# Respreading the projection's matmul pieces over the steps of a top-k search, in a hybrid attention layer

## The reference

```python
h = layer_norm(concat(meta, x))                     # 2064 x 1024
proj = h @ w_in                                     # qa ka va | qb cb | qi ki wi | gates (2 x 1024)
k_idx = layer_norm(ki); c_kv = rms_norm(cb)
rel = relu(einsum('bqhd,bsd->bqhs', qi, k_idx))     # indexer, 8 heads
score = einsum('bqh,bqhs->bqs', w_idx, rel)         # masked by chunk
top_idx = top_k(score, 256)                         # per query; then attention over those keys
y_a, y_b = window_attention(...), attention_over_gathered(...)
h = layer_norm(alpha*h + (sigmoid(gA)*y_a + sigmoid(gB)*y_b) @ w_out)
h = layer_norm(alpha*h + (silu(h @ w_gate) * (h @ w_up)) @ w_down)
```

## Time and profile before

| | |
|---|---|
| median of 3 runs | 3820.75 us (3813.96 to 3821.17) |
| the profiled execution's own time | 3810.51 us |
| its span | 3808.3 us, 2.2 us less than its time |
| granted PE clock, mean | 0.961 |
| busy share of the span: PE, PEld, DVE, ACT, POOL | 92%, 77%, 57%, 50%, 46% |

### The profile page before, as it was taken

How to read it: one execution, slowest core, us unless ns; L and a number is a source line. 1 busy time by engine, 2 the same in 40 slices (tenths; PEclk the granted TensorE clock), 3 DMA queues, 4 the chain that set the end, 5 groups by cost and what they waited for, 6 DMA issues and landing times. The chain is left out here.

```text
span 3808.3 us, 52394 instructions
## 1 busy us (share of the span) xinstructions
PE 3509.4 (92%) x17866; PEld 2927.4 (77%) x17866; DVE 2166.8 (57%) x2906; ACT 1900.5 (50%) x3569; POOL 1743.3 (46%) x2034
## 2 busy tenths in 40 slices
PE   6998788898989999999997998999999999999896
PEld 5876566676767888988996876778887888888685
DVE  4206666787522366567442665774547545466857
ACT  3213577787634698888554332343334333344342
POOL 6213566666411232222102665656665666554544
PEclk9988899899987999999998999999999999999998
DMA  7324222432231111100003455754536443465562
GB/s 249 145 71 111 79 75 70 159 84 83 83 98 39 37 40 43 35 26 15 19 15 136 148 171 200 237 194 139 180 138 202 149 149 136 153 246 188 212 226 95
DMA packets 327960, 464.22 MB, mean 122 GB/s; under 512 B 22808, under 2 KB 216552, under 8 KB 323848
## 3 DMA queue, kind: packets, MB, share of 16 engines
q1 hardware_dynamic: 301296, 417.88, 33.2%
q10 hardware_dynamic: 26400, 43.00, 3.2%
HBM read 307.02 MB, written 153.78 MB: 121 GB/s over the span
## 5 line engine op out<-in xcount | busy, mean ns | idle before, releaser
L2465 POOL TENSOR_TENSOR ff_rounded_ring<-ff_raw,ff_rounded_ring 128x512 fp32r<-128x512 f32 x264 | 383.6, 1465 | 288.2 <-ACT ff_rounded_ring L2601 285.4
L99 PE MATMUL ff_bank<-ff_rounded_pair,ff_rounded_ring 128*128 128x512 f32 x1232 | 483.2, 392 | 14.1 <-POOL ff_rounded_ring L2465 9.0
L100 PE MATMUL ff_bank<-ff_rounded_pair,ff_rounded_ring 128*128 128x512 f32 x1232 | 481.6, 391 | 0.0
L101 PE MATMUL ff_bank<-ff_rounded_pair,ff_rounded_ring 128*128 128x512 f32 x1232 | 481.6, 391 | 0.0
L1647 PE MATMUL at_ctx<-at_p_t,at_c_nat 128*128 128x128 f32 (+1 forms) x2432 | 350.7, 285 | 7.8 <-ACT at_ctx_t L1760 7.0
L1647 PEld LDWEIGHTS at_ctx<-at_p_t,at_c_nat 128*128 128x128 f32 (+1 forms) x2432 | 305.7, 194 | 37.3 <-ACT at_ctx_t L1760 12.9
L1754 ACT ACTIVATE at_p_t<-at_turn 128x512 f32<-128x512 f32 (+4 forms) x416 | 213.1, 544 | 207.0 <-PE at_turn L1624 173.5
L2470 POOL TENSOR_TENSOR ff_rounded_ring<-ff_raw,ff_rounded_ring 128x512 fp32r<-128x512 f32 x154 | 214.9, 1401 | 187.2 <-ACT ff_rounded_ring L2651 187.1
L99 PEld LDWEIGHTS ff_bank<-ff_rounded_pair,ff_rounded_ring 128*128 128x128 f32 x1232 | 232.6, 189 | 66.1 <-POOL ff_rounded_ring L2465 11.8
L2832 DVE TENSOR_TENSOR ff_rounded_a_ring<-ff_f_q,ff_rounded_a_ring 128x512 fp32r<-128x512 f32 x154 | 199.2, 1301 | 135.8 <-ACT ff_rounded_a_ring L2643 134.6
L101 PEld LDWEIGHTS ff_bank<-ff_rounded_pair,ff_rounded_ring 128*128 128x128 f32 x1232 | 232.5, 189 | 48.6
(11 more groups left out here) (360 smaller groups left out, 9106.4 us busy)
## 6 DMA issues: line engine op xcount, KB each, us to landing
f_kept<-ff_resid SPq DMA_DIRECT2D x154, 256.0 KB, 2.5
ff_f_q<-f_kept SPq DMA_DIRECT2D x14, 2816.0 KB, 10.1
pj_raw<-in_w_in SPq DMA_DIRECT2D x50, 512.0 KB, 4.5
proj<-se_row SPq DMA_DIRECT2D x96, 256.0 KB, 2.2
ff_raw<-in_w_ff_gate SPq DMA_DIRECT2D x22, 1024.0 KB, 10.7
ff_raw<-in_w_ff_up SPq DMA_DIRECT2D x22, 1024.0 KB, 6.3
ff_raw<-down_comb SPq DMA_DIRECT2D x88, 256.0 KB, 2.7
ff_raw<-in_w_ff_down SPq DMA_DIRECT2D x66, 256.0 KB, 3.2
```

The lines of the kernel that those rows point to most:

```text
L99: pe.matmul(out, lhs_lo, rhs_hi, start=start, stop=False, skip_group_check=goes_on)
L100: pe.matmul(out, lhs_hi, rhs_hi, start=False, stop=False, skip_group_check=goes_on)
L101: return pe.matmul(out, lhs_hi, rhs_lo, start=False, stop=stop, skip_group_check=goes_on)
L2465: pool.tensor_tensor(ring[:, step % RING, 1, :].rearrange("p (k c) -> p k c", c=P), f_operand(it, q, m), f32(ring[:, step % RING, 0, :]).r ...
```

## The change

The estimate of a search step's other work grows by 2600 columns for the time that hand-overs between engines take. The pause after piece 384 is one step instead of three. In the second half a step has at most 7 pieces instead of 8, except in the last eight steps. And the last two chunks of the first half are ordered by group: both units of group 2, then both of group 3.

```diff
-RELOAD_STEPS = 3
+RELOAD_STEPS = 1
...
-    units = [(c, g, k) for k, c in enumerate(OTHERS) for g in (2, 3)]
+    many = len(OTHERS)
+    units = [(c, g, k) for k, c in enumerate(OTHERS[:many - 2]) for g in (2, 3)]
+    units += [(OTHERS[k], g, k) for g in (2, 3) for k in (many - 2, many - 1)]
...
-        tally = 2 * width(2 * q + 2) + 600 if 0 <= q < LATE - 1 else 0
+        tally = 2 * width(2 * q + 2) + 3200 if 0 <= q < LATE - 1 else 0
...
-        steps[n] = range(done, done + min(many, KT))
+        steps[n] = range(done, done + min(many, KT if done < many_in_all // 2 or n > LAST_STEP - HEADS else KT - 1))
```

## The result

The changed kernel takes 3795.17 us (median of 5 runs, 3792.6 to 3799.87) against 3817.21 us for the one before, run beside it (5 runs, 3812.41 to 3821.17): a ratio of 0.995 with a 95% interval of 0.9939 to 0.9962. A second comparison gave 3797.33 against 3816.31 us, again 0.995 (0.9937 to 0.9964). It is faster by 19 to 22 us where 10 were forecast. The absolute time, 3795 us, lies just under the range of 3798 to 3825 us. That range was built on a median of 3820.75 us for the kernel before; as a share of it, it begins at 0.994, and 0.995 lies inside. The profiled execution took 3798.26 us, with a span of 3796.0.

What follows compares the result with a forecast made beforehand. PE was taken to bound steps 80 to 95, the searches round DVE, POOL and ACT steps -8 to 79. Terms -11.6 - 3 + 2.5 + 1 + 1 = -10.1 us, from 3820.75 to 3810.6 us; range 3798 to 3825 us.

Steps and rivals of the forecast that it cites:

- the main term: Steps 80 to 95 lose 17 pieces at 0.68 us with PE never idle: -11.6 us, at least zero.
- The end zone gives nothing: Rival, chance 0.05: another engine sets the pace in the last steps, or the stage's end hangs elsewhere; +1.5 us, 3822 us.
- About half should show: -3, bounds 0 and -6.1: Steps -34 to -9 lose 9 pieces, 6.1 us of PE; about half shows because ACT also waits for DVE.
- +2.5, +1 and +1: Costs forecast for units' extra ACT and POOL work, for key blocks in neighbouring steps, and for the reload's wait.
- the mark of 6 us: Sign against the forecast: the middle stretches more than 6 us longer in sum.
- the other mark: Sign against the forecast: ACT waits for PE in the middle stretches.
- Key blocks: Three pairs of key units complete in neighbouring steps, so PE waits for DVE's normalising: +1 us, bounds 0 and 6.6.
- The wait for h in step 42: PE waits 2 to 5 us for the reload's group 1, expected 13 us after issue; cost +1 us, bounds 0 and 5.
- The searches pay for the pieces: Rival, chance 0.20: POOL's 12 more quarters and ACT's copies lengthen steps -8 to 47, up to 17.8 us; +5.2 in sum, 3826 us.
- Units out of step with the loop: Rival, chance 0.10: units beginning mid-step wait for an accumulator, steps 41 to 89; at 0.6 us a step +19 us, 3840 us.
- More comes back than counted: Rival, chance 0.12: steps 48 to 79 give 5.5 us, the first stretch its whole 6.1; -18.7 us, 3802 us.

Runs made afterwards that it cites:

- key_block_earlier: Changed kernel with 8 pieces moved from steps -8 to -1 into -16 to -9, so a further key block is made before step -8; 3802.13 us, ratio 0.9984.
- pieces_earlier: Changed kernel with 6 pieces moved from steps -8 and -7 into -34 to -9, same key units completed there; 3801.96 us, ratio 0.998.
- handover_4500: As handover_and_reload, but with the estimate's constant at 4500 in place of 3200; 3767.17 us, ratio 0.9891 to the kernel before.
- all_but_order: The whole change but with the old order of the units; 3792.85 us, ratio 0.9949 to the kernel before.
- keys_apart: Changed kernel with 12 pieces moved from steps -4 to 5 into 7 to 18, so no two key units complete in neighbouring steps; 3799.82 us, ratio 0.9976.
- all_but_seven: The whole change without the limit of seven, so up to 8 pieces a step in the second half too; 3781.76 us, ratio 0.9918 to the kernel before.
- only_reload: Kernel before with only the pause shortened from three steps to one; 3804.11 us, ratio 0.998.
- handover_and_reload: Kernel before with the larger estimate and the one-step pause, old unit order, up to 8 pieces a step; 3771.63 us, ratio 0.9902.
- only_handover: Kernel before with only the larger estimate for the searches' steps (3200 in place of 600); 3783.04 us, ratio 0.9921.
- same_as_after: The changed kernel run and profiled again with no edit, beside the kernel before; 3797.33 us, ratio 0.995.

## Why the prediction was right, and where not

**The direction was right, and so was the main term.** 17 pieces fewer at the end gave 115.0 - 103.4 = 11.6 us, as forecast. It holds far beyond this case: 128, 112, 111, 88, 72 and 64 pieces take 115.0, 104.1, 103.4, 87.6, 76.7 and 71.6 us, with PE idle nowhere by more than 0.15 us. "The end zone gives nothing" is out.

**The sum is nearer than its parts.** The first stretch gave 7.2 us more than forecast, steps 48 to 79 gave 2.1 more, and the middle cost 4.3 more. These errors partly cancel, and that is luck: -15.1 us by the stretches, where -10.1 was forecast.

**The step that failed: "About half should show: -3, bounds 0 and -6.1".** Steps -34 to -9 gave 10.2 us. That is beyond its bound, because the bounds knew of pieces only. With 5 units instead of 6 a whole key block leaves the stretch, with its chain over PE, ACT, POOL and DVE. Put back with 8 pieces (key_block_earlier), the stretch takes 74.0 us, as long as before. The table of the change had the 6 and the 5. How the 10.2 us split isn't shown. At 0.65 us a piece the nine pieces would be 5.9 us and the block 4.3, but 0.65 is the most that pieces_earlier allows, and handover_4500 doesn't follow such a sum: with 3 pieces and one completed unit fewer than after, the stretch takes 70.1 us. The waits of ACT for DVE in the earlier trace rows were read as a sign that pieces are half covered; no run measures that half.

**Steps -8 to 47 cost 8.8 us, not the 4.5 forecast** (+2.5, +1 and +1). That passes the mark of 6 us that the prediction set itself, and ACT does wait for PE there (8.2 and 2.2 us), the other mark. But the largest term isn't among those named. The new order was priced at nothing and costs 8.7 us in steps 24 to 39; all_but_order, without it, is 5.2 us shorter than before there, in spite of 9 pieces more. Steps -8 to 7 cost 3.2, of which a key block moved in from the first stretch would be 3.1. Steps 8 to 23 cost 2.6 and steps 40 to 47 give 0.5. The wait that the term "Key blocks" named is there, and larger than its bound of 6.6: 9.7 us on PE for DVE's normalising, where before had 3.0. But moving the units apart didn't shorten the stretch (keys_apart), so its price of 1 us isn't confirmed. The wait for h in step 42 is 0.3 us, not 2 to 5. The load was sized fairly, 13.6 to 14.6 us from issue to landing against the 13 taken; PE came to step 42 later than forecast, after a wait of 7.1 us for line 926 at the start of step 41. What caused that one isn't shown.

**"The searches pay for the pieces"** doesn't hold. ACT's waits for POOL's judgements were 33.8 and 13.3 us, and are 32.6 and 12.6, with 12 quarters more on POOL in the middle. 39 pieces more in all_but_seven cost 7.9 us, 0.2 each, against 0.68 at the end. The 16 pieces of only_reload cost 1.3 us net, the 16 of handover_and_reload against only_handover 3.1. PE's waits for line 926 gave way, 30 us in the middle where 39 were forecast.

**"Units out of step with the loop"** was given 0.10, and its mechanism is in the trace. PE waits for the accumulator of two units earlier in 4 of the 49 steps, 10.9 us in all, hidden under "issue"; so a unit that begins within a step does meet an evacuation that ACT does at its step's end. It also waits for the next chunk's low part, an operand that the rival didn't name: 14.1 us in the middle, 8.8 in steps 48 to 79. What was wrong is the price: steps 48 to 79 got 2.1 us shorter in spite of these waits, and nothing near 0.2 us a step was lost. Steps 59 and 61, with waits of 3.5 and 4.1 us, take 11.2 and 14.0 us where before took 7.6 and 8.4, but their neighbours are shorter. Only the 6.7 of step 36 are shown to cost.

**"More comes back than counted"** (3802 us) is nearest to what happened: 2.1 us in steps 48 to 79, where its quarter was 5.5, and more than the whole 6.1 of the first stretch. 32 pieces fewer are 21.8 us of PE's work there: 12.7 of it became idle time (24.9 to 37.6), about 7 went into longer matmuls (the granted clock is 0.95 where it was 0.97), and 2.1 is gained. PE's waits for line 926 didn't rise by 20 us; they fell from 29.5 to 17.5, and waits for low parts (8.8) and for evacuations (10.9) took their place.

**What stays open.** The stretches account for -15.1 us; the ratio says 19 us, with an interval of 14.5 to 23. The difference seems to lie in the runs of before. Beside after and same_as_after their medians are 3817.21 and 3816.31 us; in the second of these comparisons eight of the nine ran at a granted clock of 0.956 to 0.958 and the ninth, at 0.961, took 3806.65 us. Beside all other versions the medians are 3809.22 to 3811.34 us, at 0.960 on average. Against those, after's two medians are 12 to 16 us faster, which fits the stretches. Why the clock was lower there isn't known. That after gains no more than this on such a chip isn't proved, since it never ran beside these. But its ratio of 0.995 shouldn't be set against the other versions' to the last 5 us.

Why the first stretch of handover_4500 takes 6.6 us longer with fewer pieces is open. Step -12 alone takes 6.2 us where after takes 1.5, with a wait of 3.7 us for line 924; before has such a wait there too. So where a block falls among the steps seems to count, not only how many there are. And what the limit of seven was for didn't show in any run: it brought waits of its own, and with the larger estimate and the shorter pause alone the kernel is faster (0.9902) than with all four parts (0.995).

## What to carry to other kernels

Where one engine sets the pace in one stretch and a loop of others in the rest, work moved out of the first is worth its whole time, and worth little where it goes (0.68 against 0.2 us a piece here), so go on moving until the last stretch has another bound; a limit that keeps work back there is paid at the full price. Count with each stretch what its units carry along, not the instructions of one engine: 8 pieces with a key block cost 10.5 us where 6 pieces cost 3.9. Don't take a wait called "issue" for a wait for nothing: look what ended just before it, and what the code waits for there. And where the order of operands' use is changed, look when the first use of each comes due and who prepares it: an operand needed one unit sooner cost as much as 13 pieces at the end, because the engine preparing it was in its own loop.

## What the runs showed of the hardware

A wait of PE can cost more than itself: after the 6.7 us of step 36 the granted clock was 0.50 in the window of 652.5 to 656.5 us, and 512-column matmuls followed at 0.43 us instead of 0.24, 2.1 us more in all. The same 0.43 us stands behind the wait of 3.47 us in step 59, and behind the 6.37 us of handover_4500, whose window of 619.8 to 623.8 us has a granted clock of 0.50. While PE stood (645.8 to 652.4 us) the searches ran on, ACT busy 6.15 of 6.60 us; in the four microseconds at half clock ACT was busy only 0.55, since it waited 3.5 us for PE's index block.

The reload moved at 415 to 426 GB/s in four windows of after with a DMA share of 0.99 to 1.15, for one core; the row of the transfer before, 424 GB/s in the earlier trace rows, was no outlier:

```profile
667.00:672.00 5.00, 5.00 (x24) 4.13 (x23) 1.85 (x3) 4.10 (x8) 1.45 (x2) 1.00 1.00 426
683.00:687.00 4.00, 3.01 (x8) 2.53 (x9) 3.34 (x6) 3.70 (x9) 3.08 (x5) 0.50 0.99 422
```

The Trainium skill's figure of about 358 GB/s for a transfer from HBM (DMA: Bandwidth & Descriptors, section Where 436 GB/s comes from) would have this reload take about a fifth longer, an estimate from 424 and 358; the rows stand against it again.
